# Late modulation chunks in the projections, and 48 of 64 prompt attention units inside the sample attention

## What is computed

```
mod = (silu(c) @ w_ada + b_ada)          # 6 x 1024: shift1, scale1, gate1, shift2, scale2, gate2
h = x * (1 + scale1) + shift1
proj = h @ w_in                          # 1024 -> 3072: qa ka va | qb kb vb, rotary on q and k
oa: 8 heads of 64, keys inside three dilated windows (a penalty table gives their weights)
ob: 4 heads, each (softmax(q1 k1) - lambda softmax(q2 k2)) v, then an RMS norm
x = layer_norm(ALPHA * x + gate1 * (concat(oa, ob) @ w_o))
u = (x * (1 + scale2) + shift2) @ w_up + b_up      # then conv, gelu, w_down, gate2, norm
```

## Time and profile before

| | us |
|---|---|
| median of 3 runs | 1243.8 |
| range | 1243.23 to 1244.69 |
| the profiled execution | 1241.13 |
| its span | 1239.0 |

### The profile page before, as it was taken

The page is one execution under the profiler, slowest core; times in us unless marked ns, Lnnn a source line. Parts: engine busy times, 40 slices in busy tenths (PEclk is TensorE's granted clock), DMA queues, the critical chain, the costliest instruction groups (busy, mean ns, idle before and its releaser), DMA issues.

```text
span 1239.0 us, 24009 instructions
## 1 busy us (share of the span) xinstructions
PE 1055.3 (85%) x9389; PEld 851.3 (69%) x9389; DVE 838.9 (68%) x1521; ACT 269.6 (22%) x588; POOL 358.1 (29%) x378
## 2 busy tenths in 40 slices
PE   4599999999577777766785996999999999999994
PEld 2377777666455545554564875999999999777772
DVE  1657457267766757685749477477676676998958
ACT  0310010232223223232333103322332232100002
POOL 2433243100000000000007005366565565434323
PEclk9799999999788679799876996999999999999997
DMA  8958894686999999999990206366567731412202
GB/s 301 403 185 303 309 370 145 215 302 225 318 325 339 313 346 302 343 331 350 301 334 17 64 26 221 121 252 238 204 221 285 269 107 69 148 56 97 73 22 77
DMA packets 112549, 276.54 MB, mean 223 GB/s; under 512 B 9608, under 2 KB 33174, under 8 KB 108837
## 3 DMA queue, kind: packets, MB, share of 16 engines
q1 hardware_dynamic: 99125, 250.82, 59.8%
q10 hardware_dynamic: 13312, 24.19, 5.5%
HBM read 264.60 MB, written 76.69 MB: 275 GB/s over the span
## 4 chain that ended last, share of the span: by engine, by line
PE 61%; DVE 21%; DMA 9%; issue 4%; SPq 3%; POOL 2%; ACT 1%; ACTq 0%; DVEq 0%; POOLq 0%; PEldq 0%
PE wide L1575 16%; PE wide L1577 15%; PE wide L1576 15%; DMA ring<-in_cache_k 5%; DVE ring L1148 5%; PE wide L1649 3%; PE wide L1638 2%; DMA ring<-in_w_ada 2%; PE wide L1700 2%; DVE ring_r L1080 2%; PE wide L1732 1%; PE wide L1524 1%; DMA ring<-in_w_down 1%; PE wide L1754 1%; PE wide L1643 1%
## 5 line engine op out<-in xcount | busy, mean ns | idle before, releaser
L744 POOL TENSOR_TENSOR ring_r<-ring,ring_r 128x1024 fp32r<-128x1024 f32 x70 | 185.2, 2654 | 271.1 <-DVE ring_r L1040 204.2
L1575 PE MATMUL wide<-x_sb_r,ring_r 128*128 128x288 f32 x704 | 211.4, 300 | 8.2 <-DVE ht_r L1062 5.1
L1576 PE MATMUL wide<-ht_r,ring_r 128*128 128x288 f32 x704 | 209.3, 297 | 0.0
L1577 PE MATMUL wide<-x_sb_r,ring_r 128*128 128x288 f32 x704 | 208.7, 296 | 0.0
L1577 PE MATMUL wide<-ring_r,ht_r 128*128 128x512 f32 (+1 forms) x400 | 158.9, 397 | 0.0
L1148 DVE STREAM_TRANSPOSE ring<-ring 128x512 f32<-128x512 f32 x208 | 129.2, 674 | 30.4 <-DMA ring<-in_cache_k 30.4
L1575 PEld LDWEIGHTS wide<-x_sb_r,ring_r 128*128 128x128 f32 x704 | 133.4, 189 | 11.7 <-issue 11.2
L1577 PEld LDWEIGHTS wide<-x_sb_r,ring_r 128*128 128x128 f32 x704 | 134.2, 191 | 0.0
L1576 PEld LDWEIGHTS wide<-ht_r,ring_r 128*128 128x128 f32 x704 | 133.7, 190 | 0.0
L1700 PE MATMUL wide<-ring,x_sb 128*32 128x128 f32 (+1 forms) x1792 | 70.2, 309 | 50.5 <-DVE ring L1148 50.4
L1575 PE MATMUL wide<-ring_r,x_sb_r 128*128 128x512 f32 (+1 forms) x240 | 97.7, 407 | 12.1 <-DVE ht_r L1062 10.1
(11 more groups left out here) (225 smaller groups left out, 1889.0 us busy)
## 6 DMA issues: line engine op xcount, KB each, us to landing
ring<-in_cache_k SPq DMA_DIRECT2D x128, 256.0 KB
out_wks<-in_cache_win_k SPq DMA_DIRECT2D x8, 4080.0 KB, 19.0
out_wvs<-in_cache_win_v SPq DMA_DIRECT2D x8, 4080.0 KB, 24.8
ring<-in_w_ada SPq DMA_DIRECT2D x12, 2048.0 KB, 10.2
ring<-in_w_up SPq DMA_DIRECT2D x22, 1024.0 KB, 7.3
ring<-in_cache_win_k SPq DMA_DIRECT2D x16, 1024.0 KB
ring<-in_w_in SPq DMA_DIRECT2D x6, 2048.0 KB, 18.5
room<-in_cache_v ACTq DMA_DIRECT2D x32, 256.0 KB
```

The costliest lines, as they stand in the source:

```text
L744: nc.gpsimd.tensor_tensor(rest, w, high.bitcast(F32), ALU.subtract).then_inc(wl_rest, 1)
L1575: nc.tensor.matmul(out, left[0], right[0], start=first, stop=False)
L1576: nc.tensor.matmul(out, left[0], right[1], start=False, stop=False)
L1577: return nc.tensor.matmul(out, left[1], right[0], start=False, stop=last)
```

## The change

- The chunks 4 to 11 of the modulation leave the list `CHUNKS` and the first part of the prompt attention. They are loaded one after the other into one buffer (`late`, in `room`) and computed before the units in `LATE_UNIT` of the projections (3, 6, 10, 13, 16, 20, 23, 26), `ada_sum` one unit later. The window copies of samples 0 to 3 are issued one by one at the units in `COPY_UNIT`.
- NU is 16: 16 prompt units stay in the first part, 48 go into the sample attention, three in each step. On PE one `prompt_step(y)` is `weigh_b(y-2)`, `turn_b(y-1)`, `scores_b(y)`; it stands at the head of a step w, after g = 0 and after g = 2. The list still begins with group 0, so 16 of the 48 are of that group.
- `qtp` (16 maps, each with 64 zero rows) becomes `qt` (8 pairs of maps); a score product contracts over 64 rows. The memset of `qtp` goes, and ACT copies a q tile in one instruction, not two.
- New key and value rows of a step have one buffer each and two semaphores. ACT loads those of step 0 before its first exponential of the first part, behind two memsets of POOL. The small tiles of the softmax no longer lie in `maskt`.

```
-CHUNKS = [("ada", i) for i in range(4)] + [("in", i) for i in range(6)] + [("ada", i) for i in range(4, 12)] \
+CHUNKS = [("ada", i) for i in range(4)] + [("in", i) for i in range(6)] \
...
+LATE_UNIT = {4: 3, 5: 6, 6: 10, 7: 13, 8: 16, 9: 20, 10: 23, 11: 26}
+COPY_UNIT = {1: (0, "k"), 4: (0, "v"), 8: (1, "k"), 11: (1, "v"), 14: (2, "k"), 18: (2, "v"), 21: (3, "k"), 24: (3, "v")}
...
-        NU = 32
+        NU = 16
         pb = pa[NU:]
+        PER = len(pb) // (2 * DB)
...
+            def load_late(ch):
+
+                if ch > 4:
+                    sp.wait_ge(ada_mm, ch)
+                src = a["w_ada"][0].rearrange("(k p) n -> p k n", p=P)
+                sp.dma_start(late, src[:, :, CH * ch:CH * ch + CH]).then_inc(late_in, 16)
...
             act.wait_ge(page_in, 16)
+            act.wait_ge(new_zero, 3)
+            act.wait_ge(rope_ok, len(rope_units))
+            act.wait_ge(pj_a, len(v_units))
+            load_new_keys(act, 0)
+            load_new_values(act, 0)
...
                 if values_by_act(w + 1, 0):
                     load_values(act, w + 1, 0)
-                probs_b(2 * w)
+                probs_b(PER * w)
+                if w:
+                    copy_b(PER * w - 1)
                 if values_by_act(w + 1, 1):
                     load_values(act, w + 1, 1)
+                probs_b(PER * w + 1)
+                copy_b(PER * w)
                 if values_by_act(w + 1, 2):
                     load_values(act, w + 1, 2)
-                copy_b(2 * w)
-                probs_b(2 * w + 1)
+                probs_b(PER * w + 2)
+                copy_b(PER * w + 1)
                 act.wait_ge(sa_pv, w + 1)
                 nc.scalar.activation(o_s[:, w, :], bk(4)[:, 0:P], ACT.Copy).then_inc(sa_o, 1)
-                copy_b(2 * w + 1)
+            copy_b(len(pb) - 1)
...
                 if last_g:
                     turn_keys(w + 1, 0)
+                mask_b(PER * w)
+                if w:
+                    out_b(PER * w - 2)
...
                 if last_g:
                     turn_keys(w + 1, 1)
+                mask_b(PER * w + 1)
                 if w:
-                    out_b(2 * w - 1)
-                mask_b(2 * w)
+                    out_b(PER * w - 1)
                 if last_g:
                     turn_keys(w + 1, 2)
+                mask_b(PER * w + 2)
+                out_b(PER * w)
                 if last_g == 4:
                     turn_keys(w + 1, 3)
-                mask_b(2 * w + 1)
                 if last_g:
                     turn_new(w + 1)
-                out_b(2 * w)
...
+            def prompt_step(y):
+
+                if y >= 2:
+                    weigh_b(y - 2)
+                if 1 <= y <= len(pb):
+                    turn_b(y - 1)
+                if y < len(pb):
+                    scores_b(y)
...
-                if w:
-                    weigh_b(2 * w - 1)
-                scores_b(2 * w)
-
+                prompt_step(PER * w)
...
-                    if g == 2:
-                        turn_b(2 * w)
-                        scores_b(2 * w + 1)
-                pe.wait_ge(new_in[w % 2], 32 * (w // 2 + 1))
+                    if g in (0, 2):
+                        prompt_step(PER * w + 1 + g // 2)
+                pe.wait_ge(vn_in, 16 * (w + 1))
```

190 lines of the change are left out of this document (100 added, 90 removed).

## The result

| | before | after |
|---|---|---|
| median of the runs | 1243.5 us (4 runs, 1241.5 to 1244.7) | 1328.4 us (4 runs, 1317.1 to 1335.7) |
| profiled execution, span | 1239.0 us | 1315.0 us (its time 1317.1, the shortest of the four) |
| ratio | | 1.068, 95% interval 1.059 to 1.076 |
| first exponential of step 0 | 318.6 us | 308.1 us |
| from there to that of step 15 | 315.1 us | 395.6 us |

A forecast was written before the change was run, and what follows sets the result against it. PE was taken to bound projections and first prompt part, transfers the sample attention's mean pace, with about 4 us slack per pair. 1241.1 - 24 + 75 + 1 = 1293, plus 2.7 to the median: 1296 us, range 1246 to 1325.

The forecast's parts named there:

- projections: Eight chunks come in on a full PE: +23.4 us; no wait taken for late loads, up to 8 us if some come late.
- first part of the prompt attention: Eight cycles become four without chunks: -46.8 us; ACT's issue +1.5, DVE's wait -3.1; step 0 taken as 24 us earlier.
- sample attention: A third prompt unit per step: even steps 30.1 us against 23.4, odd 22.2 against 18.1; 82 us, taken as +75.
- tail: Behind the last sample step: one more weighing, +1 us.
- Queries without zero halves: Score products keep their columns and so their time; memset and second copy lay beside other work: nothing.
- bound by their chain: First part of the prompt attention: if units are chain-bound once chunks no longer fill PE, up to 3 us is given back.
- rival C: Sample attention: PE granted less clock, +25 us, and late chunks behind window copies, +4, on top of 1296: 1325 us; chance 0.12.
- the issue ahead of the copy: Sample attention: ACT's DMA issue holds back its copy, costing 3.9 us per even step and 2.1 per odd, 46 us.
- The rule of the skill: Sample attention: issue time is usually small beside the DMA, so no ACT stall; set aside for a row showing 3.73 us.
- A: Sample attention: transfers stay the bound, a pair of steps stays at 41.5 us, 1221 us in all; chance 0.13.
- B: Sample attention: ACT's copy gets out before PE asks, so the stage grows by only 29 us, 1250 in all; chance 0.18.
- What would show it: Signs in the profile: full PE in projections, step 0 24 us earlier, DMA share about 0.8, PE waits 4 us, pairs 52 us.

The follow-up runs named there:

- qt_alone: Kernel before, with only the queries kept without zero halves and scores taken from 64 rows; 1254.7 us, ratio 1.011.
- after_halves: Changed kernel in its own orders, with zero halves given back to the queries of the first part's 16 units; 1320.5 us, ratio 1.063.
- n32: Changed kernel with 16 prompt units put back into the first part (32 there, two per sample step, old order of a step); 1295.3 us, ratio 1.040.
- dve_order: Changed kernel, with DVE's turns of key groups 2 and 3 ahead of the masks of a step's second and third unit; 1297.5 us, ratio 1.043.
- copies_later: Changed kernel, with the two window copies of projection units 8 and 11 issued at units 27 and 28; 1337.3 us, ratio 1.077.
- late_load: Changed kernel, with SyncE loading late chunk 7 ahead of unit 9's store and the next projection chunk; 1335.9 us, ratio 1.075.
- act_order: Changed kernel, with ACT's exponentials and copies of prompt units ahead of its issue of the next step's value pages; 1281.4 us, ratio 1.032.
- rows_128_32: n32 with score products over all 128 rows, leaving out the separation of a row pair's two heads; 1255.5 us, ratio 1.011.
- both_orders: Changed kernel with the edits of act_order and dve_order together; 1250.1 us, ratio 1.004.
- values_by_sp: Changed kernel, with every value page and window issued by SyncE instead of ACT; 1303.0 us, ratio 1.051.
- best1: Changed kernel with act_order, dve_order, copies_later, and ACT's issue of the first new rows behind the first part's exponentials; 1238.5 us, ratio 0.997.

## Why the prediction was wrong in size and right in kind

The account of the profiled executions, 1317.1 against a sum of 1293, by the prediction's own terms:

| term | forecast | measured |
|---|---|---|
| projections | +23.4 | +29.7 (PE's first score product at 266.9 instead of 237.2) |
| first part of the prompt attention | -46.8 + 1.5 - 3.1, taken so that step 0 is 24 earlier in all | -40.2 (step 0 is 10.5 earlier in all) |
| sample attention | +75 | +80.5 |
| tail | +1 | +6.0 |
| sum | +52 | +76 |

The queries' term, nothing, has no row: in the first part of the prompt attention its cost lies in that row, and what it costs in the sample attention has not been measured in the changed kernel (in qt_alone the steps took 3.0 us more).

*Queries without zero halves* is the step that failed. Four terms were too small, and this is the one whose cost the prediction had ruled out; the others it had only sized too low. The prediction said "A score product has as many columns as before, so its time stays", and booked "Nothing." At the same clock each unit takes 0.26 us more (`qt_alone`: 9.79 us for a cycle instead of 8.76). Of the widest unit's part, 0.19 us lie between the start of its scores and the start of the turn behind them (1.05 instead of 0.86). And in the first part no longer broken up by chunks PE's granted clock can stay at 0.50. The Trainium skill, "TensorEngine Tiling (Array Packing)", section "Key Properties", says that a change of the tiling mode drains TensorE. Each unit changes from 128-row products to 64-row ones and back. It gives no price; the 0.26 us a unit agree in sign, and no run here separates a drain from the rest.

From PE's first score product to step 0 the profiled execution took 41.2 us (266.9 to 308.1), where 33.0 were forecast (81.4 before, from 237.2 to 318.6, less 46.8 and 3.1, plus 1.5). `after_halves` took 35.7 (266.3 to 302.0), so 5.5 of these 8.2 us are the 64-row scores and the low clock that comes with them; in the medians, taken on two chips, it is 7.9 us. The other 2.7 us stay with 128 rows. Most of them lie at the end of the part, where PE waits three times for DVE, 2.7 us in after and 3.1 in after_halves, against once and 1.2 us before. That is the "bound by their chain" that the prediction had named with "up to 3" and taken at nothing. In the other executions the clock can cost more, up to 5.8 us for each four units (n32); dve_order, copies_later and late_load, which have the same first part, began step 0 at 322.8, 323.8 and 320.9 us. I had put the clock in rival C, and there in the sample attention. That it would move the first part, where PE is full, I had not thought of. after_halves, at 1320.5 us, comes inside the range but still lies 24.5 above the forecast: this step is not the whole miss.

*Projections.* The 23.4 us of PE work came. "I take no wait; if a few arrive late it costs up to 8 us": one came late, with 4.8 us of wait and a chunk of 3.21 instead of 1.90 us at the low clock behind it, 6.1 of the 6.3 us that are missing. The bound was right, the value taken was not. I had named the window copies in front of the load as the danger; copies_later leaves the wait at 4.6 us without them. SyncE issued that load 9.7 us after its buffer was free; late_load issues it earlier, and the wait comes back at the next chunk, so the term as a whole did not move.

*Sample attention.* The schedule written out by hand held in its order and its waits: 30.1 us forecast for an even step, 29.9 measured as the mean; 22.2 for an odd one, 22.4 measured. That the means agree to 0.2 us is in part luck. The even steps run from 28.5 to 32.7 us, and in the one shown errors of both signs meet: PE starts its waiting prompt step at 9.1 us and not at 10.5, since the issue took 2.96 us and not 3.7, and scores key group 3 at 21.9 and not at 24.5; then the end takes 6.8 us and not 5.6, with key scores of 1.94 us where I had counted 1.08. The raw sum was 82 us; the 7 us that I took off to allow for shorter takes and issues were not there, and 80.5 came. Both mechanisms are shown by the runs that take them away: the issue ahead of the copy was priced at 3.9 and 2.1 us, 46 in all, and act_order gave back 2.7 and 2.7, 40.5 in all. DVE's masks ahead of the turns had no term of their own; dve_order prices them at 34.2. Together 79.6 of the 80.5.

*The rule of the skill.* I weighed "Issuing engines are not separate DMA queues" of the Trainium skill's "DMA: Bandwidth & Descriptors" against a row, and went by the row. act_order shows that this was right here: the same issues, from the same queue, cost 40 us less where nothing urgent stands behind them.

*Tail.* I counted one weighing. But the last step has three units and no next step's keys to lie beside them, so they run one after the other. PE's sums (`L1782` before, `L1823` after) start 13.6 us behind the last step's exponential before (647.34 - 633.74) and 20.1 after (723.86 - 703.74), 6.5 later; the rest gives back 0.5. Before:

```profile
646.34 1.16 PE L1649 MATMUL wide<-room 128*128 128x128 f32 x8 [0.69 <-ACT room L869]
647.34 0.29 PE L1782 MATMUL wide<-maskt,sums 128*128 128x16 f32 x2
```

After:

```profile
720.58 1.16 PE L1690 MATMUL wide<-room 128*128 128x128 f32 x8 [0.88 <-ACT room L888]
721.58 0.60 PE L1684 MATMUL wide<-ident,room 128*128 128x128 f32 x4
722.86 1.16 PE L1690 MATMUL wide<-room 128*128 128x128 f32 x8 [0.69 <-ACT room L888]
723.86 0.29 PE L1823 MATMUL wide<-small,sums 128*128 128x16 f32 x2
```

*The rivals.* A, that transfers stay the bound, was out as its own rule said: 52.4 us for a pair against 41.5. It is what happens once both orders are mended (a DMA share of 1.00, 316.0 us for the steps). B, that the issue hides, was out too: 12 waits of PE behind ACT's copy in 310 us. C gave 1325, nearest to the time, but by another road: of what it named, the granted clock did fall in the sample attention (0.80 to 0.74) and one late chunk came late, but the sample attention took 5.5 us beyond the 75 and not 25, and the other misses lie ahead of it and behind it. The range ended there, with no place for several terms being short at once.

*What would show it.* Most signs were as written: step 0 earlier, though by 10 and not 24 us; the DMA share at 0.79; pairs 52 us apart; DVE without waits for keys; PE waiting for ACT's copy, with 1.7 us in the step shown and 2.2 in the mean of the twelve that are listed, and not 4. "PE stays full in the projections" was not: 8 of 204 us were idle, before 4 of 176.

## What to carry to other kernels

When work is put into a stage that its transfers hold, write down for each engine's queue what stands ahead of the new work's first result. Here the same 16 units cost 80 us with DMA issues and masks ahead of what other engines wait for, and 1 us with them behind, and a hand-made schedule from rows of the trace found both waits and the length of a step, which it met more closely than its single points. Don't book an edit of an operand's shape at nothing because the columns stay: look for a row with both shapes, or bound it. And a stage in which PE is full is the place where its clock is worth most.

## What the runs showed of the hardware that I had not expected

PE was busy for 80 of 80 us at a granted clock of 0.50 (n32, 270 to 350 us), the level of 1.2 GHz. The Trainium skill, "TensorE: Matmul & The Clock Gate", section "What's actually happening", says that activity releases the throttle; by the profile's busy time this stretch is as active as any, and the clock did not rise, so here the measurement stands against the plain reading. What differed in the runs at the full level was the height of the score products (rows_128_32: 64 rows to 128, and 1.00) or the modulation chunks between the units (qt_alone: 64 rows, and 1.00). All nine profiled executions with 64-row scores and no chunks fell to 0.50 at the start of this part; none of the four with 128-row scores and no chunks did. The clock came back at about 276 us in after, 278 in act_order and both_orders, 287 in values_by_sp, 301 in best1, and 312 to 314 in dve_order, copies_later and late_load, shortly before the first key scores. after and dve_order have the same program up to there, and step 0 at 308.1 and 322.8 us, which makes that stage a matter of chance worth up to 15 us. What exactly decides it is open.

The order in SyncE's queue was the other surprise: two small stores took up to 14 us there between them, as at 146.4 us in after, and a 2 MB load of a chunk waited behind them.

```profile
146.37 14.02 SPq L571 DMA_DIRECT2D out_wvp<-room  x2
160.43 0.43 SPq L534 DMA_DIRECT2D room<-in_w_ada  x1
```

The row groups two issues, and shows their stretch, not how much of it is waiting for ACT's copy of the unit between them; that too I leave open.
